# The mLSTM prompt stage: mask and key scaling on GpSimd, the state product's scaling on ScalarE

## The chip, the core and the metric

The kernel runs on one core of one Trainium2 chip. Its time is the device time of one execution in microseconds. A core has TensorE (PE, matmul), VectorE (DVE), ScalarE (ACT), GpSimd (POOL) and SyncE (SP), each with its own queue of instructions worked off in order; they are kept in step by semaphores. Matmul results go to PSUM, the rest of the data lies in SBUF.

## What is computed

The reference is one inference step of a hybrid decoder: a layer with stick-breaking attention and a state-space mixer, then a layer with dilated attention and mLSTM heads, each followed by an MLP with layer norms, for a prompt of 1024 tokens and for 64 sample tokens. The change concerns the mLSTM heads of the prompt alone: 4 heads of width 128. The reference does, per chunk of tokens:

```
log_d = where(tri, bt_t - bt_s + it_s, -inf)          # t: query token, s: key token
m_t   = max(inter, max_s(log_d))
s     = (q . k) * exp(log_d - m_t)
num   = s @ v + w_inter * (c @ q)
den   = max(abs(sum(s) + w_inter * (n . q)), exp(-m_t))
h     = num / den
c_new = w_old * c + sum_s w_s * v k^T ;  n_new = w_old * n + sum_s w_s * k
out   = sigmoid(og) * h
```

The kernel works in chunks of 128 tokens. `c` (128x128) and `n` (128) are the state that one chunk hands to the next; the final ones are outputs too.

## The kernel before, in words

The whole program is a sequence of stages, each a block in which every engine has a hand-written queue; a barrier of all engines stands between blocks. Layer 2's mLSTM projections, gate factors and the dilated attention come first; `mlstm_prompt` (L3234) works the prompt's heads, `mlstm_sample` (L3389) those of the sample tokens, and the output projection and the MLP follow.

`mlstm_prompt` takes the 1024 tokens in 8 chunks (NCK) of 128 and in each chunk the 4 heads (MH): 32 units `u = (c, h)`, chunk outermost. All factors that depend on the gates alone were made before and lie in `cols` (four columns per chunk and head: exponent bias, factor of the state product, floor of the denominator, factor of the keys) and `wold` (decay of the state). The row terms of the exponents come from DRAM: SyncE loads the 128x128 mask (0 on and below the causal line, 1e30 elsewhere) and one broadcast tile `Mall[:, c]` (128 x 4 heads x 128) per chunk.

For one unit:
- TensorE: scores `s` = keys x queries (L3272), state product `n[:, 1]` = queries x `CT` (L3282), value product `n[:, 0]` = `pT` x values (L3284; column 129 sums the weights), state update `u` = scaled keys x values (L3288), and for the unit two before, the transpose `h` of the gated output (L3294). The first four are fp32 in two passes, the transpose has one: nine passes.
- VectorE: `e` = `Mall` + mask (L3328), the weights `pT` = `s` x scale x `e` (L3338), then for the unit two before: `nm` = state product x `cols` (L3344), `nm` += value product (L3345), the state `CT` = `CT` x `wold` + `u` (L3350), the denominator in three one-element instructions (L3352 to L3354), and the gate `hg` = `nm` x 1/den x `og` (L3357).
- ScalarE: `e` = exp(bias - `e`) (L3378), the scaled keys `kw` (L3381) and the copy of the transposed head into `xT` (L3386).
- GpSimd has one instruction in the stage, L3313: it copies the dilated attention's result `cT` into `xT`, at the stage's start.

`e`, `pT`, `kw`, `nm`, `hg` and the PSUM tiles have two buffers, chosen by `u % 2`. The order is written out by hand: in step `s` VectorE masks unit `s`, finishes unit `s-2`, and makes the weights of unit `s`; TensorE does the scores of `s`, the products of `s-1`, the transpose of `s-3`; ScalarE the exponential and keys of `s`, the head copy of `s-3`. `Chain` (`step(...)`) lets VectorE wait for the result that it has just made. After the last unit the state is transposed, copied by VectorE (L3368, L3370) and stored by SyncE (L3261, L3262). Semaphores that matter: `masked` (exponent ready), `ex` (exponential), `pr` (weights), `nd` (both products), `er` (sum read), `ud` (state update in PSUM), `cu` (state written), `kwr` (keys scaled), `hr`, `ht`, `hc` (gate, transpose, head copy), `m_ld[c]` (row terms of a chunk landed).

Of the kernel before, what the change touches and what calls it, by code (L numbers as in the profile page):

```python
# [11 lines left out]
ALU = mybir.AluOpType  # L12
ACT = mybir.ActivationFunctionType
AX = mybir.AxisListType

P = 128
# [2834 lines left out]
MH, MD = 4, 128  # L2851
MW = MH * MD
MC0 = 9 * DW
NCK = SEQ // P
# [379 lines left out]
def mlstm_prompt(K, G):  # L3234

    nc, io = K.nc, K.io
    mqT, mkT, kn, ve, og, Mrow, cols, wold = (G[n] for n in ("mqT", "mkT", "kn", "ve", "og", "Mrow", "cols", "wold"))
    units = [(c, h) for c in range(NCK) for h in range(MH)]
    NU = len(units)
    W = MD + 1  # L3240
    with ExitStack() as ctx:
        sb = lambda name, shape: ctx.enter_context(nc.sbuf_tensor("mc_" + name, shape, F32))
        CT, mask, Mall = sb("CT", [P, MH, W]), sb("mask", [P, P]), sb("Mall", [P, NCK, MH, P])
        e, pT, kw, hg = (sb(n, [P, 2, P]) for n in ("e", "pT", "kw", "hg"))
        nm, den = sb("nm", [P, 2, W]), sb("den", [P, 2, 2])
        cs, ns = sb("cs", [P, MH, P]), sb("ns", [MH, P])
        s_b = [ctx.enter_context(nc.psum_tensor(f"mc_s{i}", [P, 2, P], F32)) for i in range(2)]
        n_b = [ctx.enter_context(nc.psum_tensor(f"mc_n{i}", [P, 2, W], F32)) for i in range(2)]
        u_b = [ctx.enter_context(nc.psum_tensor(f"mc_u{i}", [P, W], F32)) for i in range(2)]
        h_b = [ctx.enter_context(nc.psum_tensor(f"mc_h{i}", [P, P], F32)) for i in range(2)]  # L3250
        ld, sc, ex, er, pr, nd, hr, ht, hc, kwr, ud, cu, dv, fin, c_done, sto, c0 = (
            K.sem("mc_" + n) for n in ("ld", "sc", "ex", "er", "pr", "nd", "hr", "ht", "hc", "kw", "ud", "cu", "dv", "fin", "cd", "sto", "c0"))
        masked, dil_kept, m_ld = K.sem("mc_masked"), K.sem("mc_dk"), [K.sem(f"mc_m{c}") for c in range(NCK)]
        with nc.Block() as block:
            @block.sync
            def _(sp):
                sp.dma_start(mask[:, :], io["c_mlmask"]).then_inc(ld, 16)
                for c in range(NCK):
                    sp.dma_start(Mall[:, c], G["Mrow_kept"][:, c * P:(c + 1) * P].partition_broadcast(P)).then_inc(m_ld[c], 16)
                sp.wait_ge(fin, 2)  # L3260
                sp.dma_start(io["mlstm_c_prompt"][0, 0].rearrange("h v k -> v h k"), cs[:, :, :]).then_inc(sto, 16)  # L3261
                sp.dma_start(io["mlstm_n_prompt"][0, 0], ns[:, :]).then_inc(sto, 16)  # L3262
                sp.wait_ge(sto, 32)
# [46 lines left out]

            @block.gpsimd
            def _(p):
                p.tensor_copy(K.xT[:, 0:2, :], G["cT"][:, :, :]).then_inc(dil_kept, 1)  # L3313
                p.wait_ge(dil_kept, 1)

            @block.vector
            def _(v):
                step = Chain(v, dv)
                v.memset(CT[:, :, :].rearrange("p a b -> p (a b)"), 0.0).then_inc(c0, 1)
                v.wait_ge(ld, 16)  # L3320

                def mask_exponents(u):
                    c, h = units[u]
                    if h == 0:
                        v.wait_ge(m_ld[c], 16)
                    if u >= 2:
                        v.wait_ge(pr, u - 1)
                    v.tensor_tensor(e[:, u % 2, :], Mall[:, c, h, :], mask[:, :], ALU.add).then_inc(dv, 1)  # L3328
                    step.n += 1
                    v.wait_ge(dv, step.n)  # L3330
                    v.sem_inc(masked, 1)

                def weights(u):
                    v.wait_ge(ex, u + 1)
                    v.wait_ge(sc, u + 1)
                    if u >= 2:
                        v.wait_ge(nd, u - 1)
                    v.scalar_tensor_tensor(pT[:, u % 2, :], s_b[u % 2][:, 0, :], MD ** -0.5, e[:, u % 2, :], ALU.mult, ALU.mult).then_inc(pr, 1)  # L3338

                def outputs(u):  # L3340
                    c, h = units[u]
                    n = nm[:, u % 2, :]
                    v.wait_ge(nd, u + 1)
                    step(v.tensor_scalar(n, n_b[u % 2][:, 1, :], cols[:, c, 1, h:h + 1], None, ALU.mult))  # L3344
                    v.tensor_tensor(n, n, n_b[u % 2][:, 0, :], ALU.add).then_inc(er, 1)  # L3345
                    v.wait_ge(er, u + 1)

                    v.wait_ge(ud, u + 1)
                    v.wait_ge(c0, 1)
                    v.scalar_tensor_tensor(CT[:, h, :], CT[:, h, :], wold[:, h, c:c + 1], u_b[u % 2][:, :], ALU.mult, ALU.add).then_inc(cu, 1)  # L3350
                    d, f = den[:, u % 2, 0:1], den[:, u % 2, 1:2]
                    step(v.scalar_tensor_tensor(d, n[:, MD:W], -1.0, n[:, MD:W], ALU.mult, ALU.max))  # L3352
                    step(v.tensor_tensor(d, d, cols[:, c, 2, h:h + 1], ALU.max))
                    step(v.reciprocal(f, d))  # L3354
                    if u >= 2:
                        v.wait_ge(ht, u - 1)
                    v.scalar_tensor_tensor(hg[:, u % 2, :], n[:, 0:MD], f, og[:, c, h * MD:(h + 1) * MD], ALU.mult, ALU.mult).then_inc(hr, 1)  # L3357

                for s in range(NU + 2):
                    if s < NU:  # L3360
                        mask_exponents(s)
                    if s >= 2:
                        outputs(s - 2)
                    if s < NU:
                        weights(s)
                v.wait_ge(c_done, 2)
                for q in range(2):
                    step(v.tensor_copy(cs[:, q::2, :], s_b[q][:, :, :]))  # L3368
                v.sem_inc(fin, 1)
                v.tensor_copy(ns[:, :], h_b[0][0:MH, :]).then_inc(fin, 1)  # L3370

            @block.scalar
            def _(a):
                for s in range(NU + 3):
                    if s < NU:
                        c, h = units[s]
                        a.wait_ge(masked, s + 1)
                        a.activation(e[:, s % 2, :], e[:, s % 2, :], ACT.Exp, bias=cols[:, c, 0, h:h + 1], scale=-1.0).then_inc(ex, 1)  # L3378
                        if s >= 2:
                            a.wait_ge(ud, s - 1)  # L3380
                        a.activation(kw[:, s % 2, :], kn[:, c, h * MD:(h + 1) * MD], ACT.Copy, scale=cols[:, c, 3, h:h + 1]).then_inc(kwr, 1)  # L3381
                    if s >= 3:
                        u = s - 3
                        c, h = units[u]
                        a.wait_ge(ht, u + 1)
                        a.activation(K.xT[:, 2 + h, c * P:(c + 1) * P], h_b[u % 2][:, :], ACT.Copy).then_inc(hc, 1)  # L3386
# [408 lines left out]
```

## Time and profile before

| | us |
|---|---|
| median of 3 runs (lowest to highest) | 4092.23 (4091.68 to 4097.23) |
| span of the profiled execution | 4092.6 |
| the stage starts (its first load is issued) | 3013.88 |
| first mask add, after the first row terms landed | 3019.52 |
| last gate of the last unit starts | 3098.90 |
| the next stage's first load is issued | 3105.71 |

The page of the profile is made from one execution: it gives the busy time of each engine, the chain that ended last, and the costliest groups of instructions. The profiled execution's own time is its span, 4092.6 us, which is 0.4 us above the median. The stage of the change lasts from 3013.9 to 3105.7 us, 2.2% of the span; none of its groups is among the costly ones of the page, so that it must be read by its window. An instruction's row gives its start, its duration, and in brackets the idle time of its engine before it with what ended that idle time.

### The profile page before, as it was taken

The numbers are of one execution on the slowest core, as the hardware profiler recorded it, in microseconds if no ns is written. First come the engines' busy times: TensorE is split into PE (matmuls) and PEld (weight loads), VectorE is DVE, ScalarE is ACT, GpSimd is POOL, SyncE is SP. The second block draws the span as 40 slices with busy tenths as digits, with TensorE's granted clock in tenths as the row PEclk, the third lists the DMA queues.
The fourth block names the chain that finished last, engine by engine and source line by source line (L and its number), as shares of the span: only waits on it lengthen the run. The fifth ranks groups of instructions, "written<-read, shape, count | busy, mean of one in ns | idle before, by whom it ended". The sixth has DMA issues, their size and how long they took to land. (4 is left out here: it accounts for less than half of the span.)

```text
span 4092.6 us, 65594 instructions
## 1 busy us (share of the span) xinstructions
PE 3650.6 (89%) x25497; PEld 2955.0 (72%) x25497; DVE 1850.9 (45%) x2788; ACT 1086.9 (27%) x2327; POOL 708.2 (17%) x621
## 2 busy tenths in 40 slices
PE   7988888888788899999998999588876899999997
PEld 7965666656565799998885677256565689888895
DVE  2148564333476543334443244544045934444445
ACT  2146444444412221112113122411122221211112
POOL 0038111111100211111112111055001211111112
PEclk9999999999888999999999999689987999999998
DMA  2210899999603011111112100058302111111111
GB/s 96 75 49 1 324 407 405 404 404 404 255 2 117 13 50 51 41 41 41 41 41 98 42 27 19 14 197 291 103 22 88 62 52 41 41 41 41 51 41 65
DMA packets 220258, 470.70 MB, mean 115 GB/s; under 512 B 31625, under 2 KB 128773, under 8 KB 216918
## 3 DMA queue, kind: packets, MB, share of 16 engines
q1 hardware_dynamic: 199046, 446.50, 29.8%
q10 hardware_dynamic: 20976, 20.97, 1.6%
q8 instruction: 157, 2.57, 0.3%
q14 instruction: 79, 0.65, 0.0%
HBM read 447.51 MB, written 19.91 MB: 114 GB/s over the span
## 5 line engine op out<-in xcount | busy, mean ns | idle before, releaser
L1979 DVE TENSOR_TENSOR x<-x,f_d 128x512 f32<-128x512 f32 x576 | 392.6, 687 | 303.2 <-PE f_d L1829 282.8
L1829 PE MATMUL f_d<-f_w2h,f_hh 128*128 128x512 f32 x1024 | 408.2, 399 | 13.0 <-DVE f_w2l L1971 8.8
L1829 PE MATMUL f_d<-f_w2l,f_hh 128*128 128x512 f32 x1024 | 406.9, 397 | 0.0
L1829 PE MATMUL f_d<-f_w2h,f_hl 128*128 128x512 f32 x1024 | 406.6, 397 | 0.0
L1951 POOL TENSOR_TENSOR f_hl<-f_h,f_hh 128x364 fp32r<-128x364 f32 (+1 forms) x192 | 176.1, 924 | 1286.0 <-ACT f_hh L1915 1286.0
L1996 DVE TENSOR_TENSOR f_h<-f_h 128x364 f32<-128x364 f32 (+1 forms) x192 | 103.1, 537 | 554.7 <-ACT f_h L1909 554.6
L825 DVE COPY ss_kT<-ss_tk 128x512 f32<-128x512 f32 x256 | 177.0, 692 | 350.8 <-PE ss_tk L717 232.2
L1829 PE MATMUL f_u<-xH,f_w1h 128*128 128x364 f32 (+1 forms) x768 | 254.4, 331 | 11.7 <-DVE f_w1l L1971 11.7
L1829 PE MATMUL f_u<-xH,w1h 128*128 128x364 f32 (+1 forms) x768 | 254.2, 331 | 2.5 <-DVEq L1981 2.5
L1829 PE MATMUL f_u<-xL,f_w1h 128*128 128x364 f32 (+1 forms) x768 | 254.1, 331 | 0.0
L1829 PE MATMUL f_u<-xL,w1h 128*128 128x364 f32 (+1 forms) x768 | 254.0, 331 | 0.0
L1829 PE MATMUL f_u<-xH,f_w1l 128*128 128x364 f32 (+1 forms) x768 | 253.9, 331 | 0.0
L1829 PE MATMUL f_u<-xH,w1l 128*128 128x364 f32 (+1 forms) x768 | 253.8, 330 | 0.0
L1909 ACT ACTIVATE f_h<-f_u 128x364 f32<-128x364 f32 (+1 forms) x192 | 91.0, 474 | 583.0 <-PE f_u L1829 582.9
L1829 PEld LDWEIGHTS f_d<-f_w2h,f_hh 128*128 128x128 f32 x1024 | 193.8, 189 | 60.2 <-DVE f_w2l L1971 9.6
L1897 ACT ACTIVATE f_w2h<-w 128x2048 fp32r<-128x2048 f32 x32 | 61.4, 1918 | 645.6 <-PE f_d L1855 630.4
L717 PE MATMUL ss_tk<-ident,ss_kv 128*128 128x128 f32 x1344 | 178.6, 276 | 56.2 <-DMA ss_kv<-in_cache_sb_kv 48.4
L1829 PEld LDWEIGHTS f_d<-f_w2h,f_hl 128*128 128x128 f32 x1024 | 193.8, 189 | 46.9
L1829 PEld LDWEIGHTS f_d<-f_w2l,f_hh 128*128 128x128 f32 x1024 | 193.8, 189 | 44.8
L901 ACT ACTIVATE ss_kT<-ss_tk 128x512 f32<-128x512 f32 x256 | 154.0, 602 | 223.3 <-PE ss_tk L717 223.0
L717 PEld LDWEIGHTS ss_tk<-ident,ss_kv 128*128 128x128 f32 x1344 | 144.2, 141 | 92.2 <-issue 91.1
L891 POOL TENSOR_TENSOR ss_z<-ss_z,ss_left 128x256 f32<-128x256 f32 x128 | 89.4, 698 | 589.7 <-DVE ss_left L854 589.7
(556 smaller groups left out, 7413.6 us busy)
## 6 DMA issues: line engine op xcount, KB each, us to landing
ss_kv<-in_cache_sb_kv SPq DMA_DIRECT2D x336, 512.0 KB, 8.2
x<-in_cache_sb_kv SPq DMA_DIRECT2D x176, 512.0 KB, 8.2
w<-in_ffn_w SPq DMA_DIRECT2D x64, 1024.0 KB, 5.2
mp_qb<-mp_q SPq DMA_DIRECT2D x24, 1024.0 KB, 7.1
x<-in_x_prompt SPq DMA_DIRECT2D x16, 512.0 KB, 7.8
pe_raw<-in_w_in_even SPq DMA_DIRECT2D x8, 1024.0 KB, 6.1
mp_kc<-in_cache_dil_kv SPq DMA_DIRECT2D x8, 1024.0 KB, 6.5
mp_vc<-in_cache_dil_kv ACTq DMA_DIRECT2D x8, 1024.0 KB, 7.3
```

Of the source, the lines that this page charges most:

```text
L717: mm = pe.transpose(turn_b[j][:, c, :], kv[g % SLOTS][:, j, c * P:(c + 1) * P], K.ident[:, :])
L825: v.tensor_copy(kT[:, g % 2, :, j, :], turn_b[j][:, :, :]).then_inc(k_copied[1], 1)
L891: p.tensor_tensor(z[:, g % 3, :], z[:, g % 3, :], left[:, g % 3, 1:2 * PAGE + 1], ALU.mult).then_inc(S["weights"], 1)
L901: a.activation(kT[:, g % 2, :, j, :], turn_b[j][:, :, :], ACT.Copy).then_inc(k_copied[0], 1)
L1829: mm = pe.matmul(out, a, b, start=(n == 0), stop=(n == len(parts) - 1))
L1897: a.activation(flat(w2h[:, :, :]), raw[:, :], ACT.Copy).then_inc(w2_high, 1)
L1909: a.activation(h[:, u % HSLOTS, 0:nn], up_b[(c * UP + u) % 4][:, 0:nn], ACT.Relu).then_inc(relu, 1)
L1951: low = lambda dst, n0, n1, at: g.tensor_tensor(dst, h[:, u % HSLOTS, n0 - at:n1 - at], hh[:, c % 2, f, n0:n1].bitcast(F32), ALU.subtract)
L1979: v.tensor_tensor(K.x[0:r, t, cs], K.x[0:r, t, cs], dn_b[(c * DOWN + u) % 4][0:r, :], ALU.add).then_inc(added, 1)
L1996: v.tensor_tensor(x, x, x, ALU.mult).then_inc(squared, 1)
```

## The change

- The mask add leaves VectorE. GpSimd adds the mask to `Mall[:, c]` in place, once per chunk for all four heads (`add_mask`, 128x512), the first chunk ahead of everything, chunk `c+1` behind the key scaling of head 1 of chunk `c`. `masked` now counts chunks.
- The exponential (ScalarE) reads `Mall` instead of `e`, and itself waits for the weights of two units before (`pr`), since it writes their buffer.
- The key scaling `kw` goes from ScalarE to GpSimd, with the same wait for `ud`.
- The scaling of the state product goes from VectorE to ScalarE: in step `s` for unit `s-1`, behind `nd` and (from the third unit) `hr`; a new semaphore `n_scaled` tells VectorE, whose sum waits for it.
- The copy of `cT` into `xT` on GpSimd goes from the stage's start to its end.

```diff
--- before.py
+++ after.py
@@ -3250,6 +3250,7 @@
         h_b = [ctx.enter_context(nc.psum_tensor(f"mc_h{i}", [P, P], F32)) for i in range(2)]
         ld, sc, ex, er, pr, nd, hr, ht, hc, kwr, ud, cu, dv, fin, c_done, sto, c0 = (
             K.sem("mc_" + n) for n in ("ld", "sc", "ex", "er", "pr", "nd", "hr", "ht", "hc", "kw", "ud", "cu", "dv", "fin", "cd", "sto", "c0"))
+        n_scaled = K.sem("mc_nsc")
         masked, dil_kept, m_ld = K.sem("mc_masked"), K.sem("mc_dk"), [K.sem(f"mc_m{c}") for c in range(NCK)]
         with nc.Block() as block:
             @block.sync
@@ -3310,25 +3311,27 @@
 
             @block.gpsimd
             def _(p):
+                p.wait_ge(ld, 16)
+
+                def add_mask(c):
+                    p.wait_ge(m_ld[c], 16)
+                    p.tensor_tensor(Mall[:, c], Mall[:, c], mask[:, :].unsqueeze(1).to_broadcast([P, MH, P]), ALU.add).then_inc(masked, 1)
+
+                add_mask(0)
+                for u, (c, h) in enumerate(units):
+                    if u >= 2:
+                        p.wait_ge(ud, u - 1)
+                    p.tensor_scalar(kw[:, u % 2, :], kn[:, c, h * MD:(h + 1) * MD], cols[:, c, 3, h:h + 1], None, ALU.mult).then_inc(kwr, 1)
+                    if h == 1 and c + 1 < NCK:
+                        add_mask(c + 1)
                 p.tensor_copy(K.xT[:, 0:2, :], G["cT"][:, :, :]).then_inc(dil_kept, 1)
                 p.wait_ge(dil_kept, 1)
+                p.wait_ge(masked, NCK)
 
             @block.vector
             def _(v):
                 step = Chain(v, dv)
                 v.memset(CT[:, :, :].rearrange("p a b -> p (a b)"), 0.0).then_inc(c0, 1)
-                v.wait_ge(ld, 16)
-
-                def mask_exponents(u):
-                    c, h = units[u]
-                    if h == 0:
-                        v.wait_ge(m_ld[c], 16)
-                    if u >= 2:
-                        v.wait_ge(pr, u - 1)
-                    v.tensor_tensor(e[:, u % 2, :], Mall[:, c, h, :], mask[:, :], ALU.add).then_inc(dv, 1)
-                    step.n += 1
-                    v.wait_ge(dv, step.n)
-                    v.sem_inc(masked, 1)
 
                 def weights(u):
                     v.wait_ge(ex, u + 1)
@@ -3341,7 +3344,7 @@
                     c, h = units[u]
                     n = nm[:, u % 2, :]
                     v.wait_ge(nd, u + 1)
-                    step(v.tensor_scalar(n, n_b[u % 2][:, 1, :], cols[:, c, 1, h:h + 1], None, ALU.mult))
+                    v.wait_ge(n_scaled, u + 1)
                     v.tensor_tensor(n, n, n_b[u % 2][:, 0, :], ALU.add).then_inc(er, 1)
                     v.wait_ge(er, u + 1)
 
@@ -3357,8 +3360,6 @@
                     v.scalar_tensor_tensor(hg[:, u % 2, :], n[:, 0:MD], f, og[:, c, h * MD:(h + 1) * MD], ALU.mult, ALU.mult).then_inc(hr, 1)
 
                 for s in range(NU + 2):
-                    if s < NU:
-                        mask_exponents(s)
                     if s >= 2:
                         outputs(s - 2)
                     if s < NU:
@@ -3374,11 +3375,17 @@
                 for s in range(NU + 3):
                     if s < NU:
                         c, h = units[s]
-                        a.wait_ge(masked, s + 1)
-                        a.activation(e[:, s % 2, :], e[:, s % 2, :], ACT.Exp, bias=cols[:, c, 0, h:h + 1], scale=-1.0).then_inc(ex, 1)
+                        a.wait_ge(masked, c + 1)
                         if s >= 2:
-                            a.wait_ge(ud, s - 1)
-                        a.activation(kw[:, s % 2, :], kn[:, c, h * MD:(h + 1) * MD], ACT.Copy, scale=cols[:, c, 3, h:h + 1]).then_inc(kwr, 1)
+                            a.wait_ge(pr, s - 1)
+                        a.activation(e[:, s % 2, :], Mall[:, c, h, :], ACT.Exp, bias=cols[:, c, 0, h:h + 1], scale=-1.0).then_inc(ex, 1)
+                    if 1 <= s <= NU:
+                        u = s - 1
+                        c, h = units[u]
+                        a.wait_ge(nd, u + 1)
+                        if u >= 2:
+                            a.wait_ge(hr, u - 1)
+                        a.activation(nm[:, u % 2, :], n_b[u % 2][:, 1, :], ACT.Copy, scale=cols[:, c, 1, h:h + 1]).then_inc(n_scaled, 1)
                     if s >= 3:
                         u = s - 3
                         c, h = units[u]
```

## Rows read from the trace of the kernel before

**Rows 1.** The page, part 1: busy time of each engine.
```profile
PE 3650.6 (89%) x25497; PEld 2955.0 (72%) x25497; DVE 1850.9 (45%) x2788; ACT 1086.9 (27%) x2327; POOL 708.2 (17%) x621
```

**Rows 2.** Groups of the stage (3010 to 3103 us): busy, mean ns, idle before.
```profile
L3284 PE MATMUL mc_n<-ve,mc_pT 128*128 128x129 f32 x64 | 19.4, 394 | 26.1 <-DVE mc_pT L3338 26.1
...
L3378 ACT ACTIVATE mc_e<-mc_e,cols 128x128 f32<-128x128 f32 x32 | 12.9, 402 | 49.4 <-DVEq L3331 49.4
...
L3381 ACT ACTIVATE mc_kw<-kn,cols 128x128 f32<-128x128 f32 x32 | 12.4, 386 | 0.0
...
L3328 DVE TENSOR_TENSOR mc_e<-mc_Mall,mc_mask 128x128 f32<-128x128 f32 x32 | 9.0, 282 | 5.0 <-DMA mc_Mall<-Mrow_kept 5.0
```

**Rows 3.** The timeline of one unit at the high clock: start, us, engine.
```profile
3048.61 0.29 DVE L3338 SCALAR_TENSOR_TENSOR mc_pT<-mc_s,mc_e 128x128 f32<-128x128 f32 x1
3048.81 0.28 DVE L3328 TENSOR_TENSOR mc_e<-mc_Mall,mc_mask 128x128 f32<-128x128 f32 x1
...
3048.95 0.49 PE L3284 MATMUL mc_n<-ve,mc_pT 128*128 128x129 f32 x2 [0.91 <-DVE mc_pT L3338]
...
3049.24 0.35 DVE L3344 TENSOR_SCALAR mc_nm<-mc_n,cols 128x129 f32<-128x129 f32 x1
3049.28 0.39 PE L3288 MATMUL mc_u<-ve,mc_kw 128*128 128x129 f32 x2
...
3049.50 0.27 PE L3294 MATMUL mc_h<-ident,mc_hg 128*128 128x128 f32 x1
...
3049.63 0.29 DVE L3345 TENSOR_TENSOR mc_nm<-mc_nm,mc_n 128x129 f32<-128x129 f32 x1
...
3049.96 0.35 DVE L3350 SCALAR_TENSOR_TENSOR mc_CT<-mc_CT,wold,mc_u 128x129 f32<-128x129 f32 x1
...
3050.22 0.15 DVE L3352 SCALAR_TENSOR_TENSOR mc_den<-mc_nm 128x1 f32<-128x1 f32 x1
...
3050.80 0.35 DVE L3357 SCALAR_TENSOR_TENSOR mc_hg<-mc_nm,mc_den,og 128x128 f32<-128x128 f32 x1
3051.07 0.28 DVE L3338 SCALAR_TENSOR_TENSOR mc_pT<-mc_s,mc_e 128x128 f32<-128x128 f32 x1
```

**Rows 4.** The same timeline near the loop's start, at the low clock.
```profile
3023.42 0.64 PE L3272 MATMUL mc_s<-mqT,mkT 128*128 128x128 f32 x2
...
3025.18 0.42 PE L3294 MATMUL mc_h<-ident,mc_hg 128*128 128x128 f32 x1
...
3025.39 0.64 PE L3272 MATMUL mc_s<-mqT,mkT 128*128 128x128 f32 x2
```

**Rows 5.** Busy time and granted clock (PEclk) over the steady loop.
```profile
3020.00:3096.00 76.00, 54.21 (x278) 45.02 (x279) 65.28 (x275) 29.00 (x93) 0.00 (x0) 0.82 0.07 19
```

**Rows 6.** GpSimd instructions of other stages, by shape: busy, mean ns.
```profile
L564 POOL TENSOR_TENSOR xT<-xT,sp_l 128x511 f32<-128x511 f32 x8 | 8.7, 1087 | 5.6 <-DVE sp_l L532 3.7 <-ACT sp_z L583 1.9
...
L3313 POOL COPY xT<-cT 128x2176 f32<-128x2176 f32 x1 | 2.0, 1998 | 158.6 <-POOLq L2778 158.6
```

**Rows 7.** VectorE beside a GpSimd add, 3180 to 3195 us.
```profile
3183.98 2.98 POOL L1670 TENSOR_TENSOR x<-x,po_gb 128x1024 f32<-128x1024 f32 x1 [36.12 <-DVE x L1617]
...
3184.61 3.42 DVE L1600 TENSOR_TENSOR x<-x,po_ggb 128x1024 f32<-128x1024 f32 x1
...
3188.07 1.23 DVE L1601 TENSOR_TENSOR x<-x,po_ggb 128x1024 f32<-128x1024 f32 x1
```

**Rows 8.** VectorE beside GpSimd's scalar instruction, from 2169 us.
```profile
2169.21 15.11 POOL L1960 TENSOR_SCALAR x<-x,f_agg,f_rstd 128x1024 f32<-128x1024 f32 x4 [34.17 <-DVE f_shift L2032]
...
2175.66 0.16 DVE L2032 SCALAR_TENSOR_TENSOR f_shift<-f_agg,f_rstd 128x1 f32<-128x1 f32 x1
```

**Rows 9.** VectorE beside a GpSimd product in the dilated sample stage, the timeline.
```profile
2755.04 9.70 POOL L2979 TENSOR_TENSOR mp_prod<-mp_qb,mp_kc 128x2048 f32<-128x2048 f32 x2 [9.56 <-DVE mp_s L3175]
...
2762.49 2.27 DVE L3199 TENSOR_TENSOR mp_lse<-mp_l,mp_m 64x4 f32<-64x4 f32 x1
```

**Rows 10.** All executions of that four-element add: duration min/median/max.
```profile
L3199 DVE TENSOR_TENSOR mp_lse<-mp_l,mp_m x3: 156/2265/2272, 2762.5 to 2880.3; 64x4 f32<-64x4 f32 x3
```

## The prediction

> **What bounds the kernel now.** The page comes first: VectorE is busy 45% of the whole span and GpSimd 17% [rows 1], averages that say nothing of a stage of 93 us in 4092.6. So the second view is the groups of that stage. GpSimd has one instruction there (L3313 [rows 6]), while ScalarE's exponential sat idle 49.4 us in front of its 32 executions and TensorE 26.1 us for the weights that VectorE makes [rows 2]: both wait for VectorE. The third view is one unit in order of time [rows 3]. VectorE's weights (L3338) start at 3048.61 and again at 3051.07, a period of 2.46 us, and in between it waits for nothing but its own results. TensorE's products, the gate's transpose and ScalarE's copies lie inside that period with room. The last question is whether TensorE would bind if VectorE were faster. A unit is nine passes through the array. At the high clock the two passes of the state update start 0.22 before the transpose [rows 3], so nine take about 1.0 us; at the low clock (1.2 of 2.4 GHz), working without a gap, a whole unit takes 3025.39 - 3023.42 = 1.97 us [rows 4]. The mean granted clock over the loop is 0.82 [rows 5]; at two levels, 1.0 and 0.5, that is 36% of the time low. Today the low clock costs nothing, since 1.97 is under 2.46.
>
> **The change, part by part.** *The mask leaves VectorE.* From the weights to the mask add is 0.20 us, from there to the scaling 0.43 (VectorE waits for its own add before it signals it), from the scaling to the sum 0.39 [rows 3]. *The scaling leaves VectorE too.* The sum then follows the weights directly; I give it the 0.20 that one instruction takes to follow another there. 1.02 becomes 0.20: 0.82 less, a VectorE period of **1.64 us**, with the state update at 0.53 after the weights, the denominator at 0.79, the gate (L3357) at 1.37.
>
> *ScalarE* loses the key scaling (386 ns [rows 2]) and gains the state product's scaling. No ScalarE row here has 128x129 read from PSUM with a column scale; the nearest is the 386 ns, and between 0.28 and 0.6 the sum is the same. Exponential, scaling and head copy are some 0.9 us of issue in 1.64. The new wait stands in the queue ahead of the head copy and of the next exponential. It is for the value product: that starts 0.34 after the weights and ends 0.49 later [rows 3], so ScalarE's scaling is ready near 1.3 after the weights (1.6 at the low clock), and VectorE asks for it at 1.64 + 0.20 = 1.84. No stall, with 0.2 to 0.5 to spare. The longer loop through ScalarE (weights, value product, state update, transpose, head copy, exponential, weights two units on) is some 2 us for two units: no bound. The swap of waits on the exponential (earlier weights instead of VectorE's mask) frees it earlier.
>
> *GpSimd* gains 32 key scalings and 8 mask adds. No row has 128x128 with one scalar. The ends: by elements of the copy [rows 6], 128 / 2176 of 1998 ns, 0.12 us; by elements of the two-scalar instruction (15.11 us for four of 1024 [rows 8]), 0.47; I take 0.47, the only row with scalar columns, and let it reach 0.6. A mask add over four heads is 512 elements with two inputs: 1.09 for 511 [rows 6]; I take 1.2, up to 1.4 for the repeated operand. A chunk costs GpSimd 4 x 0.47 + 1.2 = 3.1 us of four periods (6.6): it isn't the bound. TensorE needs keys two units after GpSimd may start them, and the next chunk's mask is made two units ahead: hidden, if GpSimd isn't held. The queue past which the copy of the dilated result (1998 ns [rows 6]) is moved is GpSimd's own: it now runs behind the last key scaling, some 4 us ahead of the last gate, beside the last gates, the transposes and the state's stores. Priced at nothing; without that cover, 2.0. SyncE's queue is unchanged; its row loads have landed in time for every chunk but the first [rows 2], and the mask of the later chunks is wanted at most a few us sooner.
>
> *Edges.* The first mask add is on the path behind the first landing: 1.2 instead of 0.28, 0.9 lost. The last two units have no mask today, so they gain only the 0.39 of the scaling, 0.8 together. Net -0.1.
>
> *The shared side of GpSimd and VectorE.* A VectorE instruction with both inputs in SBUF waits for a running GpSimd instruction: L1600 takes 3.42 us, L1601 of the same shape 1.23, and L1600 ends 1.07 after the GpSimd add ends [rows 7], so 0.16 of its length passes while held. Even four elements wait: 2.27 us beside a GpSimd product that ends at 2764.74, 0.02 before them [rows 9], against 156 ns alone [rows 10]. But a one-element one took 0.16 in the middle of GpSimd's scalar instruction [rows 8], so one element, or that GpSimd form, doesn't hold. The Trainium skill ("SBUF — State Buffer", Who interferes with whom) says that a VectorE instruction with two SBUF inputs contends with any GpSimd instruction that reads SBUF, exclusively, and one with a single SBUF input does not; the first rows agree with it, the one-element row doesn't. By that rule the three two-input instructions of a unit (two of the denominator, the gate) would be held by every GpSimd instruction.
>
> Placed in the period: GpSimd may scale keys when the state update two units back is done, 0.67 + 0.39 = 1.06 after the weights [rows 3]; it runs from about 1.10 to 1.57, and the gate, due at 1.37, is held 0.20, less 0.16: 0.04. Once a chunk the mask add follows, to 2.77, which is 1.13 of the next period: the denominator, due at 0.79, is held 0.34 less 0.16, 0.18. Four times 0.04 and 0.18 is 0.34 a chunk: 0.1 a unit with rounding up. The ends are 0 (nothing held) and full serial work, 3.1 / 4 = 0.8 a unit; I stand near the lower, because of these placements. At 0.6 and 1.4 the placements give 0.2 to 0.3.
>
> *The clock.* Where it is low, TensorE sets 1.97. Today 36% of the loop is low; the engine will be busier per us, and I take a third. Period: 2/3 x 1.74 + 1/3 x 1.97 = 1.82. Thirty periods x (2.46 - 1.82) = 19.3, less 0.1: **19.2 us**. The profiled execution's span is 4092.6 and the median of the runs 4092.2, 0.4 lower; from the median, 4092.2 - 19.2 = **4073.0 us**. What follows is behind a barrier of all engines and moves up whole.
>
> **The rivals.**
> 1. *Nothing is held, clock high:* 30 x 0.82 - 0.1 = 24.5, 4067.7 us. For it: the one-element row. Against: the four-element row and the low 36%. Chance 0.22.
> 2. *TensorE is the bound throughout:* the clock stays low; 30 x (2.46 - 1.97) - 0.1 = 14.6, 4077.6 us. For it: at the start of the loop it is low with the engine working without a gap [rows 4]. Against: 0.82. Chance 0.18.
> 3. *Every GpSimd read holds the two-input instructions, beyond my placement:* a held gate delays the weights, and the pattern drifts; a period of 2.0 to 2.3 gives 4 to 14 us, 4078 to 4088. The denominator's one-element instructions would have to be held too, against [rows 8]. This is where the rule of the Trainium skill leads with the dearer GpSimd prices. Chance 0.14.
> 4. *Slower:* GpSimd and VectorE end up working by turns. At 0.6 and 1.4 a unit is 1.64 + 3.8 / 4 = 2.59, 30 x 0.13 = 4 us over, 4096 us. It decides from 0.82 us of GpSimd a unit; past 0.2% needs 1.1. For it: [rows 7], where VectorE lost the rest of GpSimd's add. Against: of VectorE's seven instructions four have one SBUF input, and run on. Chance 0.04, half of it past 0.2%.
> 5. *The change moves no bound:* the scaling comes late, since ScalarE starts it on the value product, and VectorE waits where it computed. That needs over 0.5 us more of latency than the rows show; the period is then back near 2.4, 4090 us. Chance 0.02.
> My forecast has the remaining 0.40.
>
> **The numbers.** 0.2% is 8.2 us, about what a measurement of this kernel tells from none. Forecast, rivals 1 and 2 and two thirds of rival 3 are faster by more: 0.90 (rounded). The rest of 3, rival 5 and half of 4 lie within: 0.08. Slower 0.02. The range takes in rivals 1 and 2 and the near part of 3, and a us for the runs' own spread: 4066.5 to 4081.
>
> **What would show it.** Weights start to start: 1.64 to 1.8 us at the high clock, 1.9 to 2.0 at the low one, with TensorE then without a gap. VectorE's gate longer than 0.35 in the mean where keys are scaled; its sum and weights unchanged. GpSimd 0.3 to 0.6 for keys, 1.1 to 1.4 for the mask. ScalarE's scaling with an idle time whose releaser is the value product, and no wait of VectorE for it. The first weights 0.9 later behind the landing. The prediction is wrong if VectorE's sum waits for ScalarE, if GpSimd's key scaling is over 1 us, if its last copy runs into the end, or if the stage's end doesn't move the kernel's end by as much.

## The result, and the profile after

| | before | changed |
|---|---|---|
| median of 4 runs, us | 4091.95 (4090.18 to 4097.23) | 4076.11 (4073.16 to 4077.6) |
| span of the profiled execution | 4092.6 | 4073.6 |
| the stage, its first load to the next stage's first load | 3013.88 to 3105.71: 91.8 | 3015.89 to 3088.18: 72.3 |
| loop, first to last weights | 75.0 | 55.3 |

The ratio of the two is estimated at 0.9947 with a 95% interval of 0.9935 to 0.9959; the medians alone give 0.9961, the spans 0.9954. A second set of runs on one chip gives 4077.02 against 4095.18, ratio 0.9955 (0.9942 to 0.9969). So the kernel is some 16 to 22 us faster. The stage alone says it more sharply: 91.8 - 72.3 = 19.5 us. A repeated run of the changed kernel gives 72.27, while whole runs of one kernel differ by 4 to 14 us, in part from stages ahead of this one (in the changed kernel's trace the stage itself begins 2.0 us later than before). The experiments are therefore read by the stage. The stage has two loose ends of its own: its first row terms landed 5.3 to 6.4 us after its start in the traces of all runs, and what follows the last weights took 8.9 or 9.6 us in different traces of nearly the same code. So a difference of stages is good to about 1 us, and what lies inside the loop is read from the periods, which repeat to 0.03 us.

The groups of the stage, changed kernel (3010 to 3085 us; busy, mean ns, idle before), to be read against [rows 2]:

```profile
L3324 POOL TENSOR_SCALAR mc_kw<-kn,cols 128x128 f32<-128x128 f32 x32 | 19.3, 605 | 25.3 <-PE mc_u L3289 25.3
L3285 PE MATMUL mc_n<-ve,mc_pT 128*128 128x129 f32 x64 | 16.2, 336 | 21.1 <-DVE mc_pT L3341 21.1
...
L3388 ACT ACTIVATE mc_nm<-mc_n,cols 128x129 f32<-128x129 f32 x32 | 11.8, 370 | 28.6 <-PE mc_n L3285 28.5
...
L3318 POOL TENSOR_TENSOR mc_Mall<-mc_Mall,mc_mask 128x512 f32<-128x512 f32 x8 | 10.2, 1269 | 162.3 <-DMA mc_Mall<-Mrow_kept 162.3
...
L3355 DVE SCALAR_TENSOR_TENSOR mc_den<-mc_nm 128x1 f32<-128x1 f32 x32 | 8.7, 272 | 0.0
L3356 DVE TENSOR_TENSOR mc_den<-mc_den,cols 128x1 f32<-128x1 f32 x32 | 6.0, 187 | 1.1
...
L3327 POOL COPY xT<-cT 128x2176 f32<-128x2176 f32 x1 | 2.0, 1997 | 0.0
```

TensorE's idle time for the weights is 21.1 us, from 26.1: VectorE is still the engine that the others wait for. GpSimd's key scaling takes 605 ns and its mask add 1269. And VectorE's first denominator instruction, 152 ns in every unit before, now has a mean of 272: something stretches it. Its spread says how (one tile's instructions, min/median/max):

```profile
L3355 DVE SCALAR_TENSOR_TENSOR mc_den<-mc_nm x32: 151/152/1294, 3025.5 to 3080.8; 128x1 f32<-128x1 f32 x32
L3356 DVE TENSOR_TENSOR mc_den<-mc_den,cols x32: 159/159/307, 3025.7 to 3081.0; 128x1 f32<-128x1 f32 x32
...
L3360 DVE SCALAR_TENSOR_TENSOR mc_hg<-mc_nm,mc_den,og x32: 350/352/381, 3026.1 to 3081.4; 128x128 f32<-128x128 f32 x32
```

A median of 152 and a maximum of 1294: most are free, a few are held. The gate (L3360), which I had expected to be held, is not, but for one of 381 ns. The timeline shows one free unit and one held:

```profile
3042.00 0.60 POOL L3324 TENSOR_SCALAR mc_kw<-kn,cols 128x128 f32<-128x128 f32 x1 [1.02 <-PE mc_u L3289]
...
3042.21 0.35 DVE L3360 SCALAR_TENSOR_TENSOR mc_hg<-mc_nm,mc_den,og 128x128 f32<-128x128 f32 x1
...
3042.48 0.28 DVE L3341 SCALAR_TENSOR_TENSOR mc_pT<-mc_s,mc_e 128x128 f32<-128x128 f32 x1
3042.68 0.28 DVE L3348 TENSOR_TENSOR mc_nm<-mc_nm,mc_n 128x129 f32<-128x129 f32 x1
...
3043.00 0.35 DVE L3353 SCALAR_TENSOR_TENSOR mc_CT<-mc_CT,wold,mc_u 128x129 f32<-128x129 f32 x1
...
3043.26 0.15 DVE L3355 SCALAR_TENSOR_TENSOR mc_den<-mc_nm 128x1 f32<-128x1 f32 x1
3043.35 0.37 ACT L3388 ACTIVATE mc_nm<-mc_n,cols 128x129 f32<-128x129 f32 x1 [0.73 <-PE mc_n L3285]
...
3043.63 0.60 POOL L3324 TENSOR_SCALAR mc_kw<-kn,cols 128x128 f32<-128x128 f32 x1 [1.02 <-PE mc_u L3289]
...
3043.84 0.35 DVE L3360 SCALAR_TENSOR_TENSOR mc_hg<-mc_nm,mc_den,og 128x128 f32<-128x128 f32 x1
...
3044.11 0.28 DVE L3341 SCALAR_TENSOR_TENSOR mc_pT<-mc_s,mc_e 128x128 f32<-128x128 f32 x1
3044.20 1.27 POOL L3318 TENSOR_TENSOR mc_Mall<-mc_Mall,mc_mask 128x512 f32<-128x512 f32 x1
...
3044.89 0.59 DVE L3355 SCALAR_TENSOR_TENSOR mc_den<-mc_nm 128x1 f32<-128x1 f32 x1
...
3045.44 0.61 POOL L3324 TENSOR_SCALAR mc_kw<-kn,cols 128x128 f32<-128x128 f32 x1
...
3045.52 0.30 DVE L3356 TENSOR_TENSOR mc_den<-mc_den,cols 128x1 f32<-128x1 f32 x1
...
3046.06 0.35 DVE L3360 SCALAR_TENSOR_TENSOR mc_hg<-mc_nm,mc_den,og 128x128 f32<-128x128 f32 x1
3046.33 0.28 DVE L3341 SCALAR_TENSOR_TENSOR mc_pT<-mc_s,mc_e 128x128 f32<-128x128 f32 x1
```

From weights to weights: 3042.48 to 3044.11 is 1.63 us, as worked out, with the sum 0.20 after the weights and ScalarE's scaling (3043.35) long ready when VectorE asks. The next one, 3044.11 to 3046.33, is 2.22: the mask add starts at 3044.20, ends at 3045.47, and the denominator, begun at 3044.89, ends at 3045.48 with it. The second denominator instruction is stretched too, 0.30 for 0.16, as the next key scaling starts. The weights, the sum and the state update, which run while GpSimd adds and have one of their two inputs in PSUM, keep their 0.28, 0.28 and 0.35. The long period comes six times, though GpSimd adds seven masks behind the first: the earliest of them (3023.92 to 3025.19) is over before VectorE's first denominator is due at 3025.49. The list of waits has no entry for any of it, since a held instruction counts as busy. At the end of the loop it happens once more, with the copy that was moved there:

```profile
3075.88 2.00 POOL L3327 COPY xT<-cT 128x2176 f32<-128x2176 f32 x1
...
3076.59 1.29 DVE L3355 SCALAR_TENSOR_TENSOR mc_den<-mc_nm 128x1 f32<-128x1 f32 x1
...
3078.58 0.28 DVE L3341 SCALAR_TENSOR_TENSOR mc_pT<-mc_s,mc_e 128x128 f32<-128x128 f32 x1
```

Granted clock and busy times of the loop (PE, PEld, DVE, ACT, POOL; then the clock), against [rows 5]:

```profile
3023.00:3028.00 5.00, 4.41 (x20) 4.41 (x21) 3.41 (x15) 1.96 (x7) 3.38 (x5) 0.50 0.84 208
3028.00:3079.00 51.00, 36.01 (x258) 30.65 (x256) 47.05 (x199) 25.67 (x86) 26.16 (x35) 1.00 0.00 1
3023.00:3079.00 56.00, 40.41 (x276) 35.06 (x276) 50.46 (x213) 27.62 (x92) 29.54 (x40) 0.95 0.08 20
```

The clock is at its low level in the first 5 us only, and then high to the loop's end; before, it fell back five times, for 3.3 or 6.7 us each. The unit that lies whole in the low stretch behind the start-up took 1.71 us (its transpose is not there yet, so it has eight passes), the next, at whose start the clock rises, 1.80.

### The profile page after: what moved, and what is told of

It is laid out like the page before. It is cut to its first block and busy times, and to the rows that moved or that the text cites. A ratio compares the mean times of both kernels' runs of the same rounds, so it can differ in the third digit from the quotient of the medians.

```text
span 4073.6 us, 65624 instructions
## 1 busy us (share of the span) xinstructions
PE 3637.9 (89%) x25497; PEld 2944.3 (72%) x25497; DVE 1837.6 (45%) x2724; ACT 1086.1 (27%) x2327; POOL 736.6 (18%) x661
```

## The experiments

The theory (A): the period of the loop is what VectorE issues in a unit, 1.63 us; what is lost beyond it is taken by GpSimd's instructions, which hold VectorE's instructions with two inputs in SBUF. Its rivals: that freeing ScalarE of the keys was needed; that the gain came in good part from TensorE's clock; that the long periods are something other than a hold.

### One part of the change alone

*The mask part alone*, on the kernel before:

```diff
 @block.gpsimd   (kernel before; the copy stays first)
+    p.wait_ge(ld, 16)
+    for c in range(NCK):
+        p.wait_ge(m_ld[c], 16)
+        if c >= 1: p.wait_ge(ud, MH * c - 4 + 1)
+        p.tensor_tensor(Mall[:, c], Mall[:, c], mask[:, :].unsqueeze(1).to_broadcast([P, MH, P]), ALU.add).then_inc(masked, 1)
 @block.vector
-    mask_exponents(s)
 @block.scalar
-    a.wait_ge(masked, s + 1);  a.activation(e[:, s % 2, :], e[:, s % 2, :], ACT.Exp, ...)
+    a.wait_ge(masked, c + 1);  a.wait_ge(pr, s - 1)      # from s = 2
+    a.activation(e[:, s % 2, :], Mall[:, c, h, :], ACT.Exp, ...)
```

> The kernel before with the mask part of the change alone: GpSimd adds the mask per chunk, behind the state update of the unit four before the chunk, ScalarE's exponential waits for the weights; keys stay on ScalarE, the state product's scaling on VectorE. Theory A: VectorE's period 2.46 - 0.43 = 2.03 us, and in each of 7 chunks the mask add of 1.27, begun 1.06 after the weights, holds the denominator, due at 1.18, until 2.3: 1.0 more. Stage 91.8 - 30 x 0.43 + 0.9 + 7 x 1.0 = 87 us. Rival (no hold): 79.8. Rival (ScalarE's later exponential is waited for): the weights wait for the exponential in the list of waits.

Measured: stage 86.1 us, near the 87 of theory A, periods 2.02 and six times 2.98, kernel 4085.4 in its one run. The timeline of VectorE at a chunk, and GpSimd's add beside it:

```profile
3045.72 0.28 DVE L3333 SCALAR_TENSOR_TENSOR mc_pT<-mc_s,mc_e 128x128 f32<-128x128 f32 x1
...
3046.89 0.15 DVE L3347 SCALAR_TENSOR_TENSOR mc_den<-mc_nm 128x1 f32<-128x1 f32 x1
3047.08 1.12 DVE L3348 TENSOR_TENSOR mc_den<-mc_den,cols 128x1 f32<-128x1 f32 x1
...
3048.44 0.35 DVE L3352 SCALAR_TENSOR_TENSOR mc_hg<-mc_nm,mc_den,og 128x128 f32<-128x128 f32 x1
3048.70 0.28 DVE L3333 SCALAR_TENSOR_TENSOR mc_pT<-mc_s,mc_e 128x128 f32<-128x128 f32 x1
```

```profile
3046.93 1.26 POOL L3319 TENSOR_TENSOR mc_Mall<-mc_Mall,mc_mask 128x512 f32<-128x512 f32 x1 [7.78 <-PE mc_u L3288]
```

The add starts 0.04 after the first denominator instruction, which escapes; the second waits until the add ends at 3048.19 (1.12 us for 0.16). So 0.44 of the period is the mask's, 30 x 0.44 = 13.2 us, and half of it is given back, by six holds of 0.96 and one of 0.69 on the loop's first denominator.

*The scaling part alone*, on the kernel before:

```diff
 @block.vector, outputs(u)
-    step(v.tensor_scalar(n, n_b[u % 2][:, 1, :], cols[:, c, 1, h:h + 1], None, ALU.mult))
+    v.wait_ge(n_scaled, u + 1)
 @block.scalar, behind the key scaling, for u = s - 1
+    a.wait_ge(nd, u + 1);  a.wait_ge(hr, u - 1)          # from u = 2
+    a.activation(nm[:, u % 2, :], n_b[u % 2][:, 1, :], ACT.Copy, scale=cols[:, c, 1, h:h + 1]).then_inc(n_scaled, 1)
```

> The kernel before with the scaling of the state product on ScalarE alone; mask on VectorE, keys on ScalarE, GpSimd idle in the loop. Theory A: the sum follows the mask add 0.43 after its start; period 2.46 - 0.39 = 2.07 us, no hold anywhere, stage 91.8 - 32 x 0.39 = 79.4 us. Rival (ScalarE with four instructions a unit delivers the scaling late): VectorE's sum waits for ScalarE, period over 2.1, stage over 81.

Measured: stage 81.5 us, period 2.14, where theory A had 79.4 and 2.07; 4087.3 in its one run. The rival's figures came (over 81, over 2.1), but not its reason, as the waits show:

```profile
DVE mc_nm L3346 <- DVE mc_e L3329: 6.0, 28, 0.2
...
DVE mc_nm L3346 <- ACT mc_nm L3389: 0.2, 1, 0.2
```

VectorE waits for ScalarE once in the whole loop, 0.2 us; with keys, exponential, scaling and copy in one queue ScalarE is not late. What it waits for in 28 units, 0.2 each, is its own mask add, whose end it signals before it goes on. The step from mask to sum is 0.50 here, 0.43 to the scaling before. So the scaling alone brings 0.32 a unit. The new wait for `n_scaled` stands in VectorE's queue behind that wait for the mask; whether it is what makes the 0.07, no run tells. The parts: 0.44 and 0.32 singly, 0.83 together.

### The keys on ScalarE again

```diff
 @block.gpsimd   (changed kernel; its wait for ud stays)
-    p.tensor_scalar(kw[:, u % 2, :], kn[:, c, h * MD:(h + 1) * MD], cols[:, c, 3, h:h + 1], None, ALU.mult).then_inc(kwr, 1)
 @block.scalar, behind the exponential
+    a.wait_ge(ud, s - 1)                                 # from s = 2
+    a.activation(kw[:, s % 2, :], kn[:, c, h * MD:(h + 1) * MD], ACT.Copy, scale=cols[:, c, 3, h:h + 1]).then_inc(kwr, 1)
```

> The changed kernel with the key scaling back on ScalarE, so that GpSimd has the mask adds alone. Theory A (only VectorE's queue and what holds it count; ScalarE has room): ScalarE issues some 1.2 us of 1.63, the period stays 1.63. GpSimd then runs the mask adds as early as the loads land, in the first 12 us, so the holds come early, when TensorE is the slow side, or vanish: stage 68 to 71 us. Rival C (freeing ScalarE was needed): ScalarE's queue of exponential, keys, scaling and head copy delays the scaling that VectorE waits for, period 1.8 or more, stage 75 or more, and VectorE's sum waits for ScalarE in the list of waits.

Measured: stage 74.0 us, period 1.63 in the free units, some 2.64 in four chunks (1.93 in one, 2.83 in the first), 3.28 at the copy. Rival C falls: the period doesn't need GpSimd's key scaling. The stage I expected was wrong, because GpSimd still waited for the state update at the same places, so the adds did not run early. Without a key scaling ahead of it the add starts 1.32 after the weights, 0.4 earlier in the period than in the changed kernel (1.72), and lands on the gate:

```profile
3040.02 1.26 POOL L3318 TENSOR_TENSOR mc_Mall<-mc_Mall,mc_mask 128x512 f32<-128x512 f32 x1 [6.28 <-PE mc_u L3289]
3040.07 1.37 DVE L3359 SCALAR_TENSOR_TENSOR mc_hg<-mc_nm,mc_den,og 128x128 f32<-128x128 f32 x1
...
3041.35 0.28 DVE L3340 SCALAR_TENSOR_TENSOR mc_pT<-mc_s,mc_e 128x128 f32<-128x128 f32 x1
```

The gate takes 1.37 us for 0.35. A hold costs what is left of the GpSimd instruction when VectorE's two-input instruction comes up, less the part of its own length that passes meanwhile, and that is set by where in the period it starts: 0.59 a chunk in the changed kernel, 0.96 with the mask part alone, 1.01 here. In all these runs a held one-element instruction ends 0.01 to 0.02 us behind the GpSimd add or copy, and a held gate 0.15 behind it.

### Does GpSimd's scalar form hold VectorE at all?

In the changed kernel the gate runs at 3042.21 inside a key scaling of 3042.00 to 3042.60 and takes its 0.35. First the same scaling as a product of two tensors:

```diff
-    p.tensor_scalar(kw[:, u % 2, :], kn[:, c, h * MD:(h + 1) * MD], cols[:, c, 3, h:h + 1], None, ALU.mult).then_inc(kwr, 1)
+    p.tensor_tensor(kw[:, u % 2, :], kn[:, c, h * MD:(h + 1) * MD], cols[:, c, 3, h:h + 1].to_broadcast([P, MD]), ALU.mult).then_inc(kwr, 1)
```

> The changed kernel, with the key scaling on GpSimd as a product of two tensors (the keys and their column repeated) in place of the scalar form. Theory A' (the scalar form does not hold VectorE, the two-tensor form does): the product, some 0.45 us from 1.15 after the weights, holds the gate, due at 1.37, until 1.6 less 0.16: the gate's duration rises from 0.352 to 0.4 to 0.5 in nearly every unit, period 1.65 to 1.8, stage 73 to 78 us. Rival (GpSimd's form does not matter; the gate merely falls beside it): gate 0.352, stage 72.3 or a little less for the shorter instruction.

Measured: stage 71.6 us, gate 0.352, period 1.63, the product 0.400. That settles nothing: the product is shorter than the scalar form, and it ended 0.17 after the gate began. A held gate ends 0.15 behind the release, so of its 0.35 us the first 0.20 can pass while it is held, and the product was over by then. It had to be longer. (The run hints that the hold works the other way round too: in five chunks the mask add comes up here while the gate runs, and takes 1.35 us for 1.26.) So both forms over 256 columns, with the other half unused (TensorE's state update then reads `kwx`, not shown):

```diff
+    kwx = sb("kwx", [P, 2, 2 * P]);  src = kn[:, c, min(h, 2) * MD:(min(h, 2) + 2) * MD]
-    p.tensor_scalar(kw[:, u % 2, :], kn[:, c, h * MD:(h + 1) * MD], cols[:, c, 3, h:h + 1], None, ALU.mult).then_inc(kwr, 1)
+    p.tensor_tensor(kwx[:, u % 2, :], src, cols[:, c, 3, h:h + 1].to_broadcast([P, 2 * MD]), ALU.mult).then_inc(kwr, 1)    # one run
+    p.tensor_scalar(kwx[:, u % 2, :], src, cols[:, c, 3, h:h + 1], None, ALU.mult).then_inc(kwr, 1)                       # the other
```

> The changed kernel with the key scaling on GpSimd as a product of two tensors over 256 columns, twice what is needed (two heads' keys, of which one is used), so that it surely lies over the gate. From the 128-column one (0.400 us) and the rows of 256 columns (0.64 to 0.73) I expect 0.70 us, begun 1.12 after the weights and ended at 1.82. Theory A' (a two-tensor GpSimd instruction holds VectorE's two-input gate): the gate, due at 1.36, ends 0.20 after 1.82, so lasts 0.65 instead of 0.352; period 1.9, stage 78 to 82 us. Rival (length and form do not matter to the gate): gate 0.352, period 1.63, stage 71 to 73.

> As the run before, but in the scalar form over 256 columns (0.605 for 128, so some 1.05 us, from 1.12 to 2.17 after the weights, over the gate at 1.36). Theory A' (the scalar form does not hold): gate 0.352 throughout, period 1.63 outside the mask adds; the mask add starts 0.45 later and holds the denominator longer, 1.0 instead of 0.59 a chunk: stage 75 to 76 us. Rival (every GpSimd instruction that reads SBUF holds the gate, by length): gate 1.0, period 2.3, stage over 90.

Measured: the two-tensor form, stage 78.2 us, gate median 0.530, period 1.81; the scalar form, stage 76.1, gate median 0.398, period 1.68 and 2.58 at the mask adds. One unit of the first, then of the second:

```profile
3047.31 0.61 POOL L3327 TENSOR_TENSOR mc_kwx<-kn,cols 128x256 f32<-128x256 f32 x1 [1.20 <-PE mc_u L3290]
...
3047.54 0.53 DVE L3363 SCALAR_TENSOR_TENSOR mc_hg<-mc_nm,mc_den,og 128x128 f32<-128x128 f32 x1
...
3047.99 0.28 DVE L3344 SCALAR_TENSOR_TENSOR mc_pT<-mc_s,mc_e 128x128 f32<-128x128 f32 x1
```

```profile
3047.90 0.92 POOL L3327 TENSOR_SCALAR mc_kwx<-kn,cols 128x256 f32<-128x256 f32 x1 [0.76 <-PE mc_u L3290]
...
3048.11 0.40 DVE L3363 SCALAR_TENSOR_TENSOR mc_hg<-mc_nm,mc_den,og 128x128 f32<-128x128 f32 x1
...
3048.44 0.28 DVE L3344 SCALAR_TENSOR_TENSOR mc_pT<-mc_s,mc_e 128x128 f32<-128x128 f32 x1
...
3050.03 0.93 POOL L3327 TENSOR_SCALAR mc_kwx<-kn,cols 128x256 f32<-128x256 f32 x1
3050.11 0.41 DVE L3359 TENSOR_TENSOR mc_den<-mc_den,cols 128x1 f32<-128x1 f32 x1
```

The product ends at 3047.92 and the gate 0.15 behind it: held to the end. The scalar form runs to 3048.82, but the gate ends at 3048.51, 0.05 late. Were it held until 3048.82 it would end near 3049.0. The second pair tells when the scalar form lets go: the one-element instruction ends at 3050.52, 0.49 after the scaling of 0.93 began; in the changed kernel the same pair is 3045.82 and 3045.44, 0.38 into a scaling of 0.61. So the scalar form holds as well, but for its first 0.4 to 0.5 us only and not to its end. Both kinds of instruction give the same moment of release. Over 256 columns the gate ends 0.615 after the scaling began and the one-element instruction 0.48; less the 0.15 and the 0.015 by which they end behind a release, that is 0.47 both times. Over 128 columns, in the changed kernel, the one gate that was stretched (381 ns) ended 0.508 after the scaling began and the one-element instruction 0.38, which makes 0.36 both times. That is why the changed kernel's gate is free: it comes up 0.21 into the scaling, and the 0.15 until the release is within the 0.20 that it can lose without harm. Neither theory had this. What GpSimd does in the rest of the instruction no run here shows.

### More work on VectorE, and the clock

```diff
 @block.vector, outputs(u), ahead of the state update
+    if u >= 1: v.wait_ge(pads, 3 * u)
+    for q in range(3):
+        v.scalar_tensor_tensor(pad[:, q, :], u_b[u % 2][:, 0:P], MD ** -0.5, mask[:, :], ALU.mult, ALU.mult).then_inc(pads, 1)
```

> The changed kernel with three more VectorE instructions a unit that read the state update's PSUM tile and the mask and write a scratch tile nobody reads, 0.20 to 0.28 us each: the period is set back by work that nobody waits for. Theory A (the period is VectorE's issue): 1.63 + 0.6 to 0.8, stage 72.3 + 32 x 0.6 to 0.8 = 91 to 98 us, and the granted clock of the loop, high after the first 8 us in the changed kernel, dips again as it did before (mean about 0.8). Rival B (the gain came in good part from TensorE's higher clock): the clock stays high and the stage rises by less than 15.

Measured: stage 93.3 us, free period 2.22, held 3.05; 4102.0 in its one run. Each added instruction costs its issue, 0.20. The clock over this loop:

```profile
3026.00:3101.00 75.00, 47.21 (x275) 41.15 (x275) 69.57 (x301) 27.75 (x92) 29.57 (x40) 0.86 0.05 15
```

It is lower than the changed kernel's 0.95 with the same TensorE work in a longer time, and the time added is VectorE's alone. In these runs the clock goes with the loop's pace: after the start it did not fall in the loops that took 51 to 55 us, and it fell at least once in each of those that took 57.8 or more, also in the run with the keys on ScalarE, at a free period of 1.63 (0.91 over its loop). It did not make the gain: before, at 2.46, the periods were the same at both levels, but for one of 2.65. In the changed kernel the low level did not come back after the first 5 us, so it had no chance to bind. What it would have cost, the run with the keys on ScalarE shows: from 3050.9 to 3054.2 its clock was low and TensorE had no gap, yet the three periods that lie in it or partly in it were 1.63, 1.63 and 1.74. That stretch cost 0.1 us; 1.97 a unit would have cost 0.7.

### The holds taken away

The copy back at the stage's start:

```diff
 @block.gpsimd
+    p.tensor_copy(K.xT[:, 0:2, :], G["cT"][:, :, :]).then_inc(dil_kept, 1)
     p.wait_ge(ld, 16)
     ...
-    p.tensor_copy(K.xT[:, 0:2, :], G["cT"][:, :, :]).then_inc(dil_kept, 1)
```

> The changed kernel, with the copy of the dilated result put back at the stage's start. Measured by the stage, from its first load to the next stage's first load: 91.8 us before, 72.3 changed. Theory A (GpSimd's copy, moved to the end, holds VectorE's denominator of unit 29 for 1.29 instead of 0.15 us): the one long period of 2.77 us at the end becomes 1.63, stage 71.2 us, 1.1 less. Rival (that long period is the tail's own order, the copy hidden): stage stays 72.3. If the copy at the start delayed the first mask add, the stage would rise by up to 2.

Measured: stage 71.1 us, the loop's last period 1.63 instead of 2.77, the other periods as before within 0.06. The copy cost 1.1 at the end; at the start it costs nothing, since it is over 4.4 us before the first row terms land. (These landed 0.75 later in this trace and the tail was 0.7 shorter, which cancel in the stage.) Then the mask per head as well:

```diff
-    def add_mask(c):
-        p.wait_ge(m_ld[c], 16)
-        p.tensor_tensor(Mall[:, c], Mall[:, c], mask[:, :].unsqueeze(1).to_broadcast([P, MH, P]), ALU.add).then_inc(masked, 1)
-    add_mask(0)
+    def add_mask(u):
+        c, h = units[u]
+        if h == 0: p.wait_ge(m_ld[c], 16)
+        p.tensor_tensor(Mall[:, c, h, :], Mall[:, c, h, :], mask[:, :], ALU.add).then_inc(masked, 1)
+    add_mask(0);  add_mask(1)
     ...                                                  # at the end: p.wait_ge(masked, NU)
-        if h == 1 and c + 1 < NCK: add_mask(c + 1)
+        if u + 2 < NU: add_mask(u + 2)
 @block.scalar
-    a.wait_ge(masked, c + 1)
+    a.wait_ge(masked, s + 1)
```

> As e1, and the mask is added per head and unit (128x128), two units ahead, behind each key scaling, instead of per chunk (128x512). Theory A (a mask add of 1.27 us reaches into the next period and holds the denominator, 0.59 in each of 7 chunks): a short add of about 0.4 starts behind the keys, ends before the denominator is due, and holds nothing: all periods 1.63; the first weights come 0.85 earlier since the first add is short. Stage 72.3 - 1.1 - 4.1 - 0.85 = 66.2 us, kernel about 6 us below the changed one, 4070. Rival (any two-input GpSimd add holds something in every unit): 32 times 0.1 to 0.4, stage 70 to 79. Rival (GpSimd becomes the bound: 0.6 + 0.4 + overheads): only if over 1.63.

Measured: stage 67.6 us, every period after the fifth 1.63 or 1.64. The groups:

```profile
L3328 POOL TENSOR_SCALAR mc_kw<-kn,cols 128x128 f32<-128x128 f32 x32 | 19.4, 607 | 17.5 <-PE mc_u L3289 17.5
...
L3321 POOL TENSOR_TENSOR mc_Mall<-mc_Mall,mc_mask 128x128 f32<-128x128 f32 x32 | 14.5, 455 | 4.1 <-DMA mc_Mall<-Mrow_kept 4.1
...
L3358 DVE SCALAR_TENSOR_TENSOR mc_den<-mc_nm 128x1 f32<-128x1 f32 x32 | 5.1, 159 | 0.0
```

GpSimd does more in sum (14.5 us of mask adds for 10.2) and holds next to nothing: three denominator instructions of the first units, by 0.06 to 0.15 us, and the mean is back to 159 ns. The stage is 1.4 us over what I expected. The short first add brought what was expected of it (first weights 0.92 us after it starts, 1.73 in the changed kernel), but the row terms landed 0.45 later in this trace. Of the other 0.9, 0.5 is my count of seven holds, where there are six, and the rest is slower first units (1.86 and 1.89 for 1.71 and 1.80). Against the kernel before, on one chip: 4072.39 to 4098.37, ratio 0.9938 (0.9926 to 0.995). Both versions on one other chip:

> The changed kernel again, beside the next run on the same chip: stage 72.3 us, periods of 1.63 with 2.22 once a chunk and 2.77 at the last but one.

> The version with masks per head and the copy first, again on the same chip as the changed kernel: stage 67.6 us as in its first run, and a median 3 to 6 us below the changed kernel's. Rival (the differences between runs lie elsewhere and cover it): medians within 2 us of each other.

Measured: 4077.02 (4074.32 to 4081.9, ratio 0.9955, 0.9942 to 0.9969) for the changed kernel, 4072.94 (4069.86 to 4076.29, ratio 0.994, 0.9927 to 0.9954) for this one; stages 72.3 and 66.9. The medians are 4.1 us apart as expected and the stages 5.4, of which 0.7 is the tail; the loops are 4.4 apart (55.4 and 51.0). The two intervals against before overlap a little, so the claim rests on the loop. This is the fastest version measured. The same with the keys on ScalarE was not run.

## Why the prediction was right, and where it was off

The forecast was 4073.0 in a range of 4066.5 to 4081; 4076.11 came, and in the stage 19.5 us against 19.2. Its parts did less well than their sum.

- **VectorE's period.** 1.64 forecast, 1.63 measured; the sum 0.20 behind the weights. Right. The split was off: 0.43 for the mask and 0.39 for the scaling are 0.44 and 0.32 when done singly, and 0.83 together; the 0.07 in the sum's wait behind the mask add was left open above.
- **ScalarE.** The scaling took 370 ns, near the 386 it was priced by, it idled for the value product (28.5 us in all), and VectorE waited for it once, at the start. Right. Rivals 4 (slower) and 5 fell.
- **TensorE's clock.** Mis-sized. I took a third of the loop at 1.97; it was low for 5 of 55 us, with periods of 1.71 and 1.80 at its end. Forecast: 1/3 x (1.97 - 1.74) x 30 = 2.3 us; measured, some 0.3. Rival 2 fell. The profile before did not say how the clock would respond, and "a third" was a guess near the 36%.
- **GpSimd's holds.** The mechanism was right, the place half wrong, the size too small. I charged 0.34 a chunk, from the gate 0.16 and the denominator 0.18. The gate lost nothing, because the scalar form lets go early, which [rows 8] could have told: there a VectorE instruction ran free 2.7 us into one of 3.8. I had left it open between "one element" and "that form"; one-element instructions are held (0.59 and 1.29 us). The denominator lost 0.59 a chunk: 0.44 in its first instruction, since the key scaling took 605 ns for my 470 and the mask add 1269 for 1200, and both push the add's end later; and 0.15 in its second, held by the next key scaling, which I had not counted. Over 30 periods: 3.0 us forecast, and six holds, 3.6 us, measured. Rival 1 (nothing is held) fell; of rival 3 the held one-element instructions came, but not the drift.
- **The copy.** This step failed. "Priced at nothing", with only a cover of time named: it ran beside the last gates, as stated, and held one denominator for 1.29 instead of 0.15. 1.1 us. The prediction had the rule in hand and didn't apply it to this instruction, a reader of SBUF like the others.
- **Edges.** The first weights came 7.36 us after the stage's start instead of 6.46: 0.9 later, as forecast.

What was over-charged for the clock (2.0) and under-charged for holds and copy (0.6 and 1.1) nearly cancelled, and what is left, 0.3, is the distance from 19.2 to 19.5. That the total came this near is in part luck. The Trainium skill ("SBUF — State Buffer", Who interferes with whom) was the better guide for the denominator: it makes no exception for one element, and the traces agree (1294 ns for 152). Where the Trainium skill ("SBUF — State Buffer", SBUF: two separate sides) says that whichever of the two starts first keeps the shared pair of ports for its whole instruction, the runs agree for GpSimd's adds, products and copies, and not for its scalar form: over 256 columns the gate lost 0.05 us though 0.7 of the GpSimd instruction were left.

## What to carry to other kernels

Moving elementwise work to GpSimd beside a full VectorE is paid by whatever VectorE instruction with two SBUF inputs comes up while GpSimd reads: look at which those are, even one-element ones, and at when in the period GpSimd starts. Short GpSimd instructions in the gap between two such instructions are free, one long one is not, although it is less work in sum. And a hold is not in the list of waits: it shows as a VectorE instruction whose maximum is far above its median.

## What the runs showed that I had not expected

- GpSimd's scalar form (one tensor, one column) holds VectorE for its first 0.36 of 0.61 us at 128 columns and its first 0.47 of 0.93 at 256; the two-tensor form of 0.61 us holds to its end.
- The hold seems to work both ways: mask adds that came up while VectorE's gate ran took 1.35 us for 1.26; no run was made for it.
- On GpSimd the scalar form is slower than the product with a repeated column: 605 against 400 ns at 128 columns, 923 against 612 at 256.
- TensorE's clock stayed high from 5 us into the changed kernel's loop of 55 us, and dipped in the loop of 75 us before (0.82 in the mean) and in one made as long by added VectorE work (0.86). It dipped in the loop of 58 us with the keys on ScalarE too, so the free period alone does not decide it.
